# A two-block transformer layer in fp32: branch gates moved into the stick attention, gather, merge and trunk in one phase, heads turned ahead of the scores

## The chip, the cores and the metric

The kernel runs on one core of one Trainium2 chip. TensorE (PE) multiplies matrices into PSUM; VectorE (DVE), ScalarE (ACT) and GpSimd (POOL) do the elementwise work, GpSimd on SBUF alone; SyncE's queue (SPq) issues all DMAs. The metric is the time of one execution in microseconds.

## The reference, cut to what matters

`x` has 1024 tokens of 1024 features. Only the end of the first block and the attention of the second are touched.

```python
# first block, after o_a (gated delta rule, 4 heads of 128) and o_b (stick-breaking attention, 8 heads of 64)
o_a = _rms(o_a, dn_out_gain).reshape(b, s, 512) * jax.nn.silu(z_a)
y_a = jnp.einsum('bsc,cd->bsd', o_a, w_up_a)
o_b = o_b * jax.nn.silu(z_b)
y_b = jnp.einsum('bsc,cd->bsd', o_b, w_up_b)
gates = jax.nn.sigmoid(proj[..., B_Z1:G1] + b_gate)
merged = gates[..., :1024] * y_a + gates[..., 1024:] * y_b
x = x + jnp.einsum('bsd,de->bse', merged, w_out)
# second block: z = rms_norm(x, g) @ w_in, then 8 heads of softmax attention over latents (MLA)
# and 4 heads of differential attention (two softmaxes a head, the second taken off with a weight)
```

Products keep fp32 precision by splitting both factors into a high part of a shorter format and the rest: each product is three matmuls, hi x hi, hi x lo and lo x hi. ScalarE writes `hi` (a copy into the shorter format), VectorE writes `lo` (a subtraction).

## The kernel before, in words

The program is a row of phases. A phase owns its SBUF, PSUM and semaphores; at its end all engines meet at a barrier, and only then does the next one issue its first DMA. Inside a phase, `run_stages` takes stages (classes with one generator for each engine) and a plan, a list of stage numbers: each engine runs through the same plan and takes one step of the stage named. Each engine executes its own stream in order; stages are tied by semaphores alone. A wait at the head of an engine's stream holds all that comes after it in that stream.

**The stick phase** (682 to 1049 us of the profile). `StickAttention` has 64 units, 8 token tiles j of 8 heads h; a unit's keys grow from 128 (tile 0) to 1024 (tile 7). For unit i: TensorE's `score` (L579 to L581), ScalarE's two sigmoids (L504, L507), VectorE's scan (L553) and product (L528), TensorE's transposes `flip` two steps later (L590), ScalarE's copy into `weight_t` (L517), TensorE's `apply` (L603). `give` copies the tile's outputs out of PSUM (L535), which are stored to `o_b`. Between the units, by `even_plan`, `GateProjection` computes the merge gates (L717 to L719, 16 weight tiles of 4 steps of 12 matmuls of 512 columns) and stores `gates`. It has one raw weight buffer; a tile's split (L678, L697) stands three steps ahead of its use.

**The gather phase** (1050 to 1117). Two rounds of four token tiles. Each loads `o_a`, `o_b`, `z_a`, `z_b`, normalises and gates them (L1484 to L1525: square, sum, square root, reciprocal, four products, SiLU), transposes them on TensorE (L1539), and splits them into `branches` (L1492, L1530).

**The merge phase** (1117 to 1221). `project_merge` goes over 4 chunks of 256 output features with both up projections, `features_products` (L186): 384 matmuls of 512 columns, two in a row with the same weights. Gates are multiplied in over all 1024 tokens (L1604), added (L1606), split (L1585, L1611) into `merged`.

**The trunk phase** (1221 to 1530). `WeightRing` streams weights through two raw and two split slots (L2466, L2474, L2479); `OutProject` (through `token_products`, L2521 to L2523) multiplies `merged` with `w_out`, token tile by token tile; `InProject` and the latents follow.

**The attend phase** (1531 to 1914). `attention_plan` interleaves two units of `MlaAttention` with one of `DiffAttention`. Both share two PSUM slots `t` for transposes and two slots `z` for scores. In a step TensorE does `score`, then `turn` (the next tile's queries or keys transposed into a `t` slot, L2020 and L375), `flip` (transposes of the softmax of two units ago, L2040 and L2322; a unit of more than 512 keys takes both `t` slots), and `apply`. Of a turned slot ScalarE writes the high part (L1880, L385) and, in `DiffAttention`, VectorE the rest (`keep_lo`, L398 and L401), which frees it. VectorE's `top` (L1963, L2241) takes the maximum and frees `z`.

Of the kernel before, what the change touches and what calls it, by code (L numbers as in the profile page):

```python
# [16 lines left out]
P = 128  # L17
# [42 lines left out]
def slot_loop(eng, n, step, straight=False):  # L60

    rounds = (n - 1) // 2
    if rounds >= 2 and not straight:
        with eng.Fori(0, rounds) as t:
            for s in range(2):
                step(t, s, True)
    else:
        for t in range(rounds):  # L70
            for s in range(2):
                step(t, s, True)
    for c in range(2 * rounds, n):
        step(c // 2, c % 2, c + 1 < n)


# [3 lines left out]


class WeightStore:

    def __init__(self, nc, stack, name, size):
        sb = lambda n, w, dtype: stack.enter_context(nc.sbuf_tensor(f"{name}_{n}", [P, w], dtype))
        self.raw = sb("w_raw", size, F32)
        self.hi = [sb(f"w_hi{s}", size, F32R) for s in range(2)]
        self.lo = [sb(f"w_lo{s}", size, F32R) for s in range(2)]  # L90

    def views(self, kt, width, pieces):
        view = lambda t: t[:, 0:kt * width].rearrange("p (k n) -> p k n", n=width)
        raw, kp = view(self.raw), kt // pieces
        return [raw[:, h * kp:(h + 1) * kp] for h in range(pieces)], [view(t) for t in self.hi], [view(t) for t in self.lo]


class Weights:

    def __init__(self, ph, kt, width, source, pieces=2, store=None, ready=False, following=None, goes_on=None):
        self.nc, self.width, self.pieces, self.source = ph.nc, width, pieces, source
        self.kp = kt // pieces
        if store:
            self.raw, self.hi, self.lo = store.views(kt, width, pieces)
        else:
            self.raw = [ph.sb(f"w_raw{h}", [P, self.kp, width])[:] for h in range(pieces)]  # L110
            self.hi = [ph.sb(f"w_hi{s}", [P, kt, width], F32R)[:] for s in range(2)]
            self.lo = [ph.sb(f"w_lo{s}", [P, kt, width], F32R)[:] for s in range(2)]

        self.goes_on = goes_on
        if goes_on:
            self.loaded, self.hi_done, self.lo_done, self.used, self.before = (
                goes_on.loaded, goes_on.hi_done, goes_on.lo_done, goes_on.used, goes_on.before)
        else:
            self.loaded = ph.sem2("w_loaded", pieces)
            self.hi_done = ph.sem2("w_hi_done", pieces)  # L120
            self.lo_done = ph.sem2("w_lo_done", pieces)
            self.used = ph.sem2("w_used")
            self.before = 1 if ready else 0
        self.next = None
        if following:
            kt, width, first = following
            self.next = Weights(ph, kt, width, lambda c, h: first(0, h), pieces, store, goes_on=self)

    def load(self, sp, t, s, width=None):
        w = width or self.width  # L130
        for h in range(self.pieces):
            if not isinstance(t, int) or 2 * t + s > self.before:

                for other in (range(self.pieces) if self.goes_on else (h,)):
                    sp.wait_ge(self.lo_done[other], 2 * t + s - self.before)
            source = self.source(2 * t + s, h) if w == self.width else self.source(2 * t + s, h, w)
            sp.dma_start(self.raw[h][:, :, 0:w], source).then_inc(self.loaded[h], 16)

    def split_hi(self, act, t, s, width=None):
        w = width or self.width  # L140
        act.wait_ge(self.used[s], t)
        for h in range(self.pieces):
            act.wait_ge(self.loaded[h], 16 * (2 * t + s + 1 - self.before))
            k = slice(h * self.kp, (h + 1) * self.kp)
            self.nc.scalar.activation(self.hi[s][:, k, 0:w], self.raw[h][:, :, 0:w],
                                      ACT.Copy).then_inc(self.hi_done[h], 1)

    def split_lo(self, dve, t, s, width=None):
        w = width or self.width
        for h in range(self.pieces):  # L150
            dve.wait_ge(self.hi_done[h], 2 * t + s + 1 - self.before)
            k = slice(h * self.kp, (h + 1) * self.kp)
            self.nc.vector.tensor_tensor(self.lo[s][:, k, 0:w], self.raw[h][:, :, 0:w],
                                         self.hi[s][:, k, 0:w].bitcast(F32),
                                         ALU.subtract).then_inc(self.lo_done[h], 1)

    def begin(self, do, eng, width=None):

        if not self.before:
            do(eng, 0, 0, width)  # L160

    def stream(self, more):

        return self if more else self.next

    def wait_split(self, pe, t, s):
        if isinstance(t, int) and 2 * t + s < self.before:
            return
        for h in range(self.pieces):
            pe.wait_ge(self.lo_done[h], 2 * t + s + 1 - self.before)  # L170

def next_item(t, s):

    return (t, 1) if s == 0 else (t + 1, 0)

def features_products(nc, out, hi, lo, w_hi, w_lo, kt, ch):  # L180

    for k in range(kt):
        for weight, part, first in ((w_hi, hi, True), (w_hi, lo, False), (w_lo, hi, False)):
            for half in range(2):
                cols = slice(half * HALF, (half + 1) * HALF)
                last = nc.tensor.matmul(out[:, cols], weight[:, k, ch], part[:, k, cols],  # L186
                                        start=(k == 0 and first), stop=(k == kt - 1 and weight is w_lo))
    return last
# [221 lines left out]
class StickAttention:  # L410
# [4 lines left out]
    def __init__(self, ph, nc, src, v, q_gain, k_gain, out, c):  # L415
        self.nc, self.v, self.out, self.c = nc, v, out, c
# [39 lines left out]
    def sync(self, sp):  # L456
# [8 lines left out]
        for i in range(self.steps()):  # L465
            if self.next_tile(i, 0) is not None:
                self.prep.load(sp, self.next_tile(i, 0))
            if i >= len(self.units):
                yield
                continue  # L470
            j, h = self.units[i]
            if h == 5 and j:
                store(j - 1)
            yield
# [46 lines left out]
    def vector(self, dve):  # L521
# [101 lines left out]
class GateProjection:  # L623
# [21 lines left out]
    def sync(self, sp):  # L645
        def load(i):
            if i:
                sp.wait_ge(self.lo_done, i)
# [25 lines left out]
    def split_hi(self, act, i):  # L674
        act.wait_ge(self.loaded, 16 * (i + 1))
        if i >= 2:
            act.wait_ge(self.summed, 2 * (i - 1))
# [3722 lines left out]
```

## Time and profile before

| | us |
|---|---|
| median of 3 runs (lowest, highest) | 2894.46 (2893.68, 2897.53) |
| the profiled execution, its own time | 2896.21 |
| its span, first to last instruction | 2894.5 |
| busy in the span: PE, DVE, ACT, POOL | 2618.9, 1267.4, 947.8, 278.1 |
| mean granted TensorE clock | 0.955 of full |

All times of the profile are counted from the start of its span. A row of the timeline is: start, duration, engine, line, operation, out<-in, shape, count, and in brackets the idle time of the engine before it and what ended it. Durations of matmuls overlap (a 512-column matmul lasts 0.39 us and the next one starts 0.23 us after it), so the pace is read from the starts. A row of busy time by stretch is: start and end, length, then busy us and instructions of TensorE, of its weight loads, of VectorE, ScalarE and GpSimd, the granted TensorE clock, the share of the DMA engines, GB/s. A row of a group is: line, engine, operation, out<-in, shape, count | busy us, mean ns | idle us before it and what ended it. A row of waits is: who waited for whom, us in total, times, longest.

### The profile page before, as it was taken

To read this page: it belongs to the slowest core of one execution; us is meant where nothing else is said; L and a number is where in the kernel's file an instruction comes from. 1 tells how busy PE (TensorE), PEld (TensorE's weight loads), DVE (VectorE), ACT (ScalarE), POOL (GpSimd) and SP (SyncE) were. 2 spreads that over 40 slices of the span, in tenths; PEclk is the share of its full clock that TensorE was granted. 3 is DMA by queue.
4 is the path that set the end of the run, shared out by engine and by line. 5 is a ranking of instruction groups with operands and counts; after the bars stand their busy time and mean duration, and the time that the engine had idled before them with its cause. 6 is when DMAs were issued, how large, how long until landed. Compare 5 with 4: busy or idle time off the path is not lost. (4 is left out here: it accounts for less than half of the span.)

```text
span 2894.5 us, 36626 instructions
## 1 busy us (share of the span) xinstructions
PE 2618.9 (90%) x14702; PEld 2245.7 (78%) x14702; DVE 1267.4 (44%) x1770; ACT 947.8 (33%) x1539; POOL 278.1 (10%) x393
## 2 busy tenths in 40 slices
PE   8969999995999955799994888979999999999999
PEld 6859999995888844688893676768788888888877
DVE  5523444432566544434124866645323323333443
ACT  4223222211456532123112766633211111122331
POOL 1002222210001000001002312111000000000000
PEclk9989999997999987999995998989999999999999
DMA  4231212102322124343235111034321221255532
GB/s 139 81 99 57 77 50 61 56 27 83 92 67 64 47 77 142 119 151 118 82 110 173 43 37 49 17 134 142 84 74 66 76 77 51 84 202 180 184 104 84
DMA packets 220256, 264.71 MB, mean 91 GB/s; under 512 B 54677, under 2 KB 153621, under 8 KB 220089
## 3 DMA queue, kind: packets, MB, share of 16 engines
q1 hardware_dynamic: 220088, 262.38, 28.4%
q8 instruction: 117, 1.92, 0.3%
q14 instruction: 51, 0.41, 0.0%
HBM read 185.11 MB, written 77.22 MB: 91 GB/s over the span
## 5 line engine op out<-in xcount | busy, mean ns | idle before, releaser
L3590 PE MATMUL ffn_up_acc<-mixed_hi,ffn_ring_hi 128*128 128x512 f32 x704 | 274.3, 390 | 2.5 <-DVE mixed_lo L2742 2.5
L3590 PE MATMUL ffn_up_acc<-mixed_hi,ffn_ring_lo 128*128 128x512 f32 x704 | 273.9, 389 | 0.0
L3590 PE MATMUL ffn_up_acc<-mixed_lo,ffn_ring_hi 128*128 128x512 f32 x704 | 273.9, 389 | 0.0
L1419 PE MATMUL delta_acc<-delta_w_hi,xn_hi 128*128 128x256 f32 x640 | 191.5, 299 | 2.9 <-DVE delta_w_lo L1373 2.9
L1421 PE MATMUL delta_acc<-delta_w_hi,xn_lo 128*128 128x256 f32 x640 | 181.1, 283 | 0.0
L1420 PE MATMUL delta_acc<-delta_w_lo,xn_hi 128*128 128x256 f32 x640 | 180.9, 283 | 0.0
L2521 PE MATMUL trunk_acc<-trunk_ring_hi,merged_hi 128*128 128x512 f32 (+1 forms) x384 | 149.7, 390 | 16.1 <-DVE trunk_ring_lo L2479 16.1
L3590 PEld LDWEIGHTS ffn_up_acc<-mixed_hi,ffn_ring_hi 128*128 128x128 f32 x704 | 132.1, 188 | 30.1 <-issue 2.9
L3590 PEld LDWEIGHTS ffn_up_acc<-mixed_hi,ffn_ring_lo 128*128 128x128 f32 x704 | 132.1, 188 | 27.6
L3590 PEld LDWEIGHTS ffn_up_acc<-mixed_lo,ffn_ring_hi 128*128 128x128 f32 x704 | 132.1, 188 | 27.2
L2522 PE MATMUL trunk_acc<-trunk_ring_lo,merged_hi 128*128 128x512 f32 (+1 forms) x384 | 147.8, 385 | 0.0
L2523 PE MATMUL trunk_acc<-trunk_ring_hi,merged_lo 128*128 128x512 f32 (+1 forms) x384 | 147.6, 384 | 0.0
L3849 DVE TENSOR_TENSOR ffn_feed_lo<-ffn_feed_raw,ffn_feed_hi 128x1536 fp32r<-128x1536 f32 x44 | 77.4, 1759 | 147.1 <-ACT ffn_feed_hi L3841 147.1
L3560 DVE TENSOR_SCALAR ffn_conv<-ffn_padded,ffn_taps 128x1024 f32<-128x1024 f32 x22 | 16.6, 753 | 274.8 <-ACT ffn_padded L3541 274.8
L1419 PEld LDWEIGHTS delta_acc<-delta_w_hi,xn_hi 128*128 128x128 f32 x640 | 122.0, 191 | 8.9 <-issue 5.5
L1420 PEld LDWEIGHTS delta_acc<-delta_w_lo,xn_hi 128*128 128x128 f32 x640 | 122.1, 191 | 0.0
L1421 PEld LDWEIGHTS delta_acc<-delta_w_hi,xn_lo 128*128 128x128 f32 x640 | 121.8, 190 | 0.0
L3541 ACT ACTIVATE ffn_padded<-ffn_up_acc 128x1024 f32<-128x1024 f32 x22 | 22.6, 1028 | 301.4 <-PE ffn_up_acc L3590 301.4
L553 DVE TENSOR_TENSOR_SCAN stick_keep<-stick_keep,stick_zero 128x127 f32<-128x127 f32 (+7 forms) x64 | 86.7, 1354 | 78.3 <-ACT stick_keep L504 77.7
L3841 ACT ACTIVATE ffn_feed_hi<-ffn_feed_raw 128x1536 fp32r<-128x1536 f32 x44 | 65.4, 1487 | 159.5 <-PE ffn_up_acc L3917 159.5
L717 PE MATMUL stick_g_acc<-xn_hi,stick_g_hi 128*128 128x512 f32 x256 | 107.3, 419 | 6.0 <-DVE stick_g_lo L697 5.6
L3917 PE MATMUL ffn_up_acc<-ffn_feed_hi 128*128 128x512 f32 x352 | 108.8, 391 | 0.0
(431 smaller groups left out, 6236.2 us busy)
## 6 DMA issues: line engine op xcount, KB each, us to landing
ffn_feed_raw<-in_w_down SPq DMA_DIRECT2D x44, 512.0 KB, 4.1
ffn_ring_raw<-in_w_gate SPq DMA_DIRECT2D x11, 1024.0 KB, 5.4
ffn_ring_raw<-in_w_up SPq DMA_DIRECT2D x11, 1024.0 KB, 5.8
scratch_act_t<-ffn_silu SPq DMA_DIRECT2D x22, 512.0 KB, 2.6
ffn_feed_raw<-scratch_act_t SPq DMA_DIRECT2D x44, 256.0 KB, 3.0
delta_w_raw<-in_w_in SPq DMA_DIRECT2D x20, 512.0 KB, 4.0
scratch_projected<-delta_out SPq DMA_DIRECT2D x80, 128.0 KB, 1.7
stick_g_raw<-in_w_in SPq DMA_DIRECT2D x16, 512.0 KB, 4.5
```

Source lines behind the costliest of these rows:

```text
L553: nc.vector.tensor_tensor_scan(back, back, self.zero[:].to_broadcast([P, n - 1]), 1.0, ALU.mult, ALU.add).then_inc(self.scanned, 1)
L717: nc.tensor.matmul(self.acc[:], w_hi, self.hi[:, k, cols], start=(k == 0), stop=False, skip_group_check=True)
L1419: nc.tensor.matmul(acc, self.hi[:, k, tok], w_hi, start=(k == 0), stop=False, skip_group_check=True)
L1420: nc.tensor.matmul(acc, self.hi[:, k, tok], w_lo, start=False, stop=False, skip_group_check=True)
L1421: last = nc.tensor.matmul(acc, self.lo[:, k, tok], w_hi, start=False, stop=(k == self.kt - 1), skip_group_check=True)
L2521: nc.tensor.matmul(out, hi[:, k, tok], w_hi, start=(k == 0), stop=False)
L2522: nc.tensor.matmul(out, hi[:, k, tok], w_lo, start=False, stop=False)
L2523: last = nc.tensor.matmul(out, lo[:, k, tok], w_hi, start=False, stop=(k == kt - 1))
L3590: last = nc.tensor.matmul(self.acc[s][:, br, cols], weight[:, k, ch], part[:, k, cols], start=(k == 0 and first), stop=(k == 7 and weight ...
L3841: self.nc.scalar.activation(self.hi[s][:], self.raw[s][:], ACT.Copy).then_inc(self.hi_done[s], 1)
L3849: self.nc.vector.tensor_tensor(self.lo[s][:], self.raw[s][:], self.hi[s][:].bitcast(F32), ALU.subtract).then_inc(self.lo_done[s], 1)
L3917: last = nc.tensor.matmul(t.pairs[j][:, half, :], part, weight[:, HALF + half * HALF:HALF + (half + 1) * HALF], start=begins, stop=ends, s ...
```

## The change

Three edits.

1. **Gates inside the stick phase.** `BranchGates`, a third stage, runs 8 steps for each token tile beside the stick's 8 units. It normalises and gates `o_a` mostly on GpSimd, and leaves `silu(z_b)` in the stick's output tile, with which `give` multiplies the output. Both halves go to one tensor `gated`. SiLU becomes a sigmoid and a product. `even_plan` puts its step behind each stick step. The stick's store moves from unit 5 to unit 4. `GateProjection` gets two raw buffers that lie on its `lo` buffers; its loads wait for the tile before to be summed, and the split stands two steps ahead of its use.
2. **One trunk phase.** `BranchGather` (load `gated`, transpose, split), `MergeWeights` (the up weights, through the ring's buffers) and `Merge` (16 units: half of the tokens by 128 features, both branches) replace the two phases, ahead of the trunk's stages. Behind merge units 12 and 13 (of 0 to 15) stand the ring's first two splits. `TokenHalves` lets later tensors take the place of dead halves; `turn` has two slots instead of one.
3. **Turn first.** In both attentions, TensorE's `turn`, ScalarE's `keep` and (`DiffAttention`) VectorE's `keep_lo` move to the front of the step.

```diff
@@ StickAttention.vector, give
-            if j:
-                dve.wait_ge(self.stored, 16 * j)
-            nc.vector.tensor_copy(self.o_sb[:], self.o[:]).then_inc(self.o_out, 1)
+            dve.wait_ge(self.gates.silu_b, j + 1)
+            nc.vector.tensor_tensor(self.o_sb[:], self.o_sb[:], self.o[:], ALU.mult).then_inc(self.o_out, 1)
@@ GateProjection.sync
         def load(i):
-            if i:
-                sp.wait_ge(self.lo_done, i)
+            if i >= 2:
+                sp.wait_ge(self.summed, 2 * (i - 1))
@@ BranchGates (new): scalar, vector, gpsimd; s is the step in the tile
+                if s == 0:
+                    act.wait_ge(self.o_in, 16 * (j + 1))
+                    if j:
+                        act.wait_ge(self.silu_b, j)
+                    nc.scalar.activation(self.sig[:], self.per_head(), ACT.Square).then_inc(self.squared, 1)
+                if s == 2:
+                    act.wait_ge(self.z_a_in, 16 * (j + 1))
+                    act.wait_ge(self.summed, j + 1)
+                    nc.scalar.activation(self.sig[:], self.z[:], ACT.Sigmoid).then_inc(self.sig_a, 1)
+                if s == 5:
+                    act.wait_ge(self.z_b_in, 16 * (j + 1))
+                    nc.scalar.activation(self.sig[:], self.z[:], ACT.Sigmoid).then_inc(self.sig_b, 1)
...
+                if s == 1:
+                    self.nc.vector.tensor_reduce(self.total[:], ...).then_inc(self.summed, 1)
...
+                if s == 1:   # GpSimd: mean and power -0.5 of 128x4, then two products of 128x512
+                if s == 3:   # two products of 128x512
+                if s == 6:   # one product of 128x512, z * sig into the stick's o_sb
@@ even_plan
-        plan.append(0)
+        plan += [0, 2]
@@ Merge.tensor (new), a unit (half, j)
+            for branch in range(2):
+                key = ("merge", u, branch)
+                self.acc.wait_free(pe, key)
+                for k in range(4):
+                    nc.tensor.matmul(out, w_hi[:, k, ch], hi, start=(k == 0), stop=False)
+                    nc.tensor.matmul(out, w_hi[:, k, ch], lo, start=False, stop=False)
+                    last = nc.tensor.matmul(out, w_lo[:, k, ch], hi, start=False, stop=(k == 3))
+                self.acc.fill(last, key)
@@ merge_plan (new), ahead of trunk_plan
+    plan = [gather, gather, weights, gather, weights, gather]
+    for u in range(16):
+        plan += [weights, weights] * (u in (0, 2, 4))
+        plan += [weights] * (u == 8)
+        plan += [gather] * (4 <= u < 8)
+        plan += [merge]
+        plan += [ring] * (u in (12, 13))
+    return plan + [merge]
@@ MlaAttention.tensor, DiffAttention.tensor
-            if i < self.nu:
-                score(i)
             for s in range(2):
                 ...
                     turn(...)
+            if i < self.nu:
+                score(i)
```

`BranchGather.sync` issues tile 0, tile 1, the first weights, tile 2, the second weights; tile 3 waits until tile 0 is transposed (three buffers). `Merge.vector` does two products of 128x512 with the sums, an addition and, one unit later, the subtraction.

## Rows read from the trace of the kernel before

**Rows 1.** The page's section on DMA issues: KB each, us to landing.

```profile
ffn_feed_raw<-in_w_down SPq DMA_DIRECT2D x44, 512.0 KB, 4.1
```

**Rows 2.** Busy time by stretch; clock in parts of full speed.

```profile
711.00:1046.00 335.00, 328.88 (x1986) 285.82 (x1986) 192.73 (x191) 173.91 (x303) 20.47 (x12) 0.99 0.22 63
1046.00:1231.00 185.00, 100.30 (x450) 83.94 (x449) 84.99 (x97) 50.12 (x57) 0.10 (x1) 0.79 0.36 128
1231.00:1527.00 296.00, 294.41 (x1383) 251.87 (x1384) 88.02 (x108) 66.17 (x125) 16.75 (x49) 0.99 0.35 119
1574.00:1912.00 338.00, 292.98 (x1912) 242.68 (x1912) 222.34 (x604) 215.87 (x501) 77.17 (x116) 0.95 0.13 36
```

**Rows 3.** TensorE in order of time, 1045 to 1239 us.

```profile
1045.65 0.39 PE L719 MATMUL stick_g_acc<-xn_hi,stick_g_lo 128*128 128x512 f32 x1
...
1125.49 1.19 PE L186 MATMUL merge_acc<-branches_hi,merge_w_hi 128*128 128x512 f32 x2 [11.12 <-DVE merge_w_lo L153]
...
1214.18 0.61 PE L186 MATMUL merge_acc<-branches_hi,merge_w_lo 128*128 128x512 f32 x2
1230.94 0.80 PE L2521 MATMUL trunk_acc<-trunk_ring_hi,merged_hi 128*128 128x512 f32 x1 [16.15 <-DVE trunk_ring_lo L2479]
...
1235.91 0.40 PE L2521 MATMUL trunk_acc<-trunk_ring_hi,merged_hi 128*128 128x512 f32 x1
...
1238.67 0.39 PE L2521 MATMUL trunk_acc<-trunk_ring_hi,merged_hi 128*128 128x512 f32 x1
```

**Rows 4.** SyncE's queue and ScalarE in order of time, behind the stick attention.

```profile
1050.43 0.33 SPq L1470 DMA_DIRECT2D gather_gain<-in_dn_out_gain  x1
...
1059.28 0.63 ACT L1484 ACTIVATE gather_square<-gather_o 128x512 f32<-128x512 f32 x1 [2.06 <-DMA gather_z<-scratch_projected]
```

**Rows 5.** Groups by line and shape, 1046 to 1231 us.

```profile
L1530 DVE TENSOR_TENSOR branches_lo<-gather_t,branches_hi 128x1024 f32 x8 | 9.4, 1219 | 3.9 <-ACT branches_hi L1492 3.9
...
L1492 ACT ACTIVATE branches_hi<-gather_t 128x1024 f32 x8 | 7.9, 1023 | 11.3 <-PE gather_t L1539 11.3
...
L1501 DVE TENSOR_REDUCE gather_stat<-gather_square 128x4 f32<-128x512 f32 x8 | 5.5, 686 | 32.6 <-ACT gather_square L1484 32.6
...
L2474 ACT ACTIVATE trunk_ring_hi<-trunk_ring_raw 128x2048 fp32r<-128x2048 f32 x2 | 3.8, 1909 | 8.0 <-DMA trunk_ring_raw<-in_w_out 8.0
...
L2479 DVE TENSOR_TENSOR trunk_ring_lo<-trunk_ring_raw,trunk_ring_hi 128x2048 fp32r<-128x2048 f32 x1 | 2.3, 2292 | 7.9 <-ACT trunk_ring_hi L2474 7.9
```

**Rows 6.** The stick attention in order of time: TensorE, SyncE's queue, ScalarE.

```profile
694.24 1.97 PE L375 MATMUL stick_t<-ident,stick_prep_xn 128*128 128x128 f32 x8 [15.82 <-DVE stick_prep_xn L365]
...
708.38 0.42 SPq L649 DMA_DIRECT2D stick_g_raw<-in_w_in  x1
...
713.87 1.06 ACT L678 ACTIVATE stick_g_hi<-stick_g_raw 128x1024 fp32r<-128x1024 f32 x1 [1.81 <-DMA stick_g_raw<-in_w_in]
```

**Rows 7.** Single lines, shortest, median, longest ns: VectorE beside GpSimd.

```profile
L1140 DVE TENSOR_TENSOR delta_upper<-delta_mt,delta_mask x8: 681/1090/1091, 233.3 to 598.3; 128x512 f32<-128x512 f32 x8
...
L1142 DVE TENSOR_TENSOR delta_upper<-ident,delta_upper x8: 693/1664/1670, 234.0 to 599.4; 128x512 f32<-128x512 f32 x8
...
L1161 POOL TENSOR_TENSOR delta_bt<-delta_mt,delta_mask x40: 1260/1286/1744, 225.8 to 621.6; 128x512 f32<-128x512 f32 x40
```

**Rows 8.** GpSimd's groups by shape: a power of 128x4.

```profile
L3393 POOL TENSOR_TENSOR ffn_mixed_inverse<-ffn_mixed_mean,ffn_mixed_half 128x4 f32<-128x4 f32 x8 | 8.1, 1011 | 0.7
```

**Rows 9.** What TensorE waited for, 1574 to 1912 us.

```profile
PE attend_mla_acc L2053 <- DVE attend_mla_o L1975: 10.7, 7, 2.1
...
PE attend_t L2322 <- DVE attend_diff_prep_k L401: 9.4, 6, 2.1
PE attend_t L2322 <- DVE attend_diff_prep_q_lo L398: 8.4, 6, 1.8
```

**Rows 10.** TensorE in the attention, waits in a long and a short tile.

```profile
1713.04 0.55 PE L2322 MATMUL attend_t<-ident,attend_diff_probs 128*128 128x128 f32 x3 [1.51 <-DVE attend_diff_prep_q_lo L398]
...
1598.45 0.88 PE L2030 MATMUL attend_z<-attend_mla_k_t,attend_mla_q_t 96*128 96x384 f32 x2 [1.07 <-DVE attend_diff_neg_top L2241]
```

More of the change, by code:

```diff
@@ L98 @@
[L98 to L170, printed above, removed]
@@ L174, in next_item @@
[L174 to L188, printed above, removed]
@@ L660, in sync @@
         for i, half, part in self.walk():
-            if half == 1 and part == 0 and i + 2 < self.tiles:
-                load(i + 2)
+            if half == 0 and part == 1 and 2 <= i + 1 < self.tiles:
+                load(i + 1)
             if part == 0 and 2 * i + half >= 1:
@@ L683, in scalar @@
         for i, half, part in self.walk():
-            if half == 0 and part == 1 and i + 1 < self.tiles:
+            if half == 1 and part == 0 and i + 1 < self.tiles:
                 self.split_hi(act, i + 1)
@@ L702, in vector @@
         for i, half, part in self.walk():
-            if half == 0 and part == 1 and i + 1 < self.tiles:
+            if half == 1 and part == 0 and i + 1 < self.tiles:
                 self.split_lo(dve, i + 1)
@@ L1633, with merge_plan @@
+def merge_plan():
+    gather, weights, merge, ring = range(8, 11), None, None, 0
+    gather, weights, merge = 8, 9, 10
+    plan = [gather, gather, weights, gather, weights, gather]
[6 more added lines that the diff above has]
+    return plan + [merge]
 MLA_H, NOPE, ROPE, MLA_V, Q_RANK, KV_RANK = 8, 64, 32, 64, 256, 128
@@ L1903, in scalar @@
         for i in range(self.steps()):
+            for s in range(2):
+                if self.following(i, 3 * s, 1) is not None:
+                    keep(self.following(i, 3 * s, 1), s)
             if self.following(i, 1) is not None:
@@ L2218, in scalar @@
         for i in range(self.steps()):
+            for s in range(2):
+                if self.following(i, s, 1) is not None:
+                    keep_hi(self.following(i, s, 1), s)
             if self.following(i, 0) is not None:
@@ L2222, in scalar @@
                 weigh(i - 1)
-            for s in range(2):
-                if self.following(i, s, 1) is not None:
-                    keep_hi(self.following(i, s, 1), s)
             if 0 <= i - 2 < self.nu:
@@ L2284, in vector @@
                 give(self.units[u][0])
+            for s in range(2):
+                if self.following(i, s, 1) is not None:
+                    self.prep.keep_lo(dve, self.following(i, s, 1), s)
             if i < self.nu:
@@ L2288, in vector @@
                 invert(i - 1)
-            for s in range(2):
-                if self.following(i, s, 1) is not None:
-                    self.prep.keep_lo(dve, self.following(i, s, 1), s)
             if self.following(i, 0) is not None:
@@ L2760, with __init__ @@
     N = 4
-    def __init__(self, ph, nc, acc):
-        self.nc, self.acc, self.tiles, self.number = nc, acc, [ph.sb(f"out{b}", [P, HALF]) for b in range(self.N)], {}
+    def __init__(self, ph, nc, acc, place):
+        self.nc, self.acc, self.tiles, self.number = nc, acc, [place.sb(f"out{b}", [P, HALF]) for b in range(self.N)], {}
         self.stored = ph.sem2("stored", self.N)
```

580 lines of the change are left out of this document (327 added, 253 removed).

## The prediction

> **What bounds the kernel now.** I read the page first: a span of 2894.5 us, and TensorE busy in 90% of it. An average over stages does not say what one stage is worth, so the next view is busy time by stretch [rows 2]. In the stick attention (711 to 1046) TensorE is busy 328.9 of 335 us, in the trunk (1231 to 1527) 294.4 of 296: both are TensorE's, and work of other engines there costs only if it stops TensorE. Between them, 1046 to 1231, TensorE is busy 100.3 of 185 us. In the attention (1574 to 1912) it is 293.0 of 338. These two stretches are where the change can win. The third view is TensorE's order of time [rows 3]: the stick's last matmul ends at 1046.0, the merge's first starts at 1125.49, its last two at 1214.18, the trunk's first at 1230.94. So the stretch is a gap of 79.4 us (64 transposes lie in it), 89.3 us of matmuls, and a gap that the bracket puts at 16.15 us and ends with the ring's `lo`. The fourth view is what TensorE waited for in the attention [rows 9].
>
> **Term 1, the gap behind the stick attention.** What stays is the barrier: the last matmul ended at 1046.0, and the first DMA of the next phase went out at 1050.43 [rows 3, 4]; after the change this DMA is tile 0 of `gated`. What goes: squares, sums, roots, products and SiLU of both rounds, the second round's loads, and the merge phase's own start. What comes is a chain of four tiles and two weight pieces of 512 KB each. A load of 512 KB lands in 4.1 us [rows 1]. When loads are queued, the next square of the gather came after 2.06 us of idle time and the 0.63 of the one before, for 1 MB of its tiles [rows 4]: 1.35 us for each further 512 KB. Eight transposes at the low clock took 1.97 us [rows 6]; a `hi` of 128x1024 takes 1.02 and a `lo` 1.22 [rows 5]; I add 0.1 for each hand-over.
> Tile 0 lands at 1054.5, is transposed at 1056.5, has its `hi` at 1057.7 and its `lo` at 1059.0. Tile 1 is transposed at 1058.5, its `lo` ends at 1061.0. The first weights follow (`lo` at 1062.2), then tile 2, which needs tile 0's slot (transposed at 1061.1, `lo` at 1063.6), then the second weights (1064.8). Tile 3's load is issued at 1056.5 behind three others and lands at about 1061.3; transposed at 1063.5, `hi` at 1064.7, `lo` at 1066.0. The first merge matmul starts at 1066.2. Bounds: VectorE's six `lo` in a row from 1057.8 end at 1065 even if no load holds, and if tile 3's load takes double the time it is 1071.
>
> **Term 2, the merge.** The same 384 matmuls of 512 columns. They came every 0.23 us, two with the same weights; now each has its own, as in the trunk, where twelve took 2.76 us, 0.230 each [rows 3]. I take 0.232: 89.1 us. The transposes of tiles 4 to 7 stand between units, 32 at half of the low clock's price [rows 6]: 3.9 us. The start at the low clock: the trunk's first twelve took 4.97 us instead of 2.76 [rows 3], 2.2 us too much (the granted clock of the whole stretch is 0.79 [rows 2], so parts of it ran at the lower level, 1.2 GHz). Sum 95.2 us, end at 1161.4. What could hold it: a unit is 24 matmuls, 5.6 us. VectorE's unit is four passes of 128x512 of 0.69 (the length of L1501 [rows 5]): 2.8 us. In units 4 to 7 a `lo` of 1.22 comes on top and in unit 4 two more, 6.5 us at most against 6.5 with the transposes, and four accumulators lie between. ScalarE has half of that. If VectorE did hold units 4 to 7 by 1 us each, it is 4 us.
>
> **Term 3, the gap ahead of the trunk.** It goes: the ring's first splits (`hi` 1.91, `lo` 2.29 [rows 5]) are ordered behind merge units 12 and 13. Counted from the end of unit 12: VectorE's products and sum 2.2, `hi` to 4.8, `lo` to 7.2; the next pair to 15.0. The trunk's first product can start at 16.8 and needs the second piece 2.8 later. Behind this `lo` on SyncE's queue stands the load of the last unit's gates: issued at 15.1, landed by 19, used at 19. The trunk's first four token tiles, 22 us, need the first half of the tokens only, so the last unit's `hi` and `lo` have cover; without it they would cost 5 us. The trunk's own start at the low clock, 2.2 us, goes too.
> So the trunk's matmuls are ahead by 1230.94 + 2.2 - 1161.4 = 71.7 us. From there the trunk is TensorE's, and does the same.
>
> **Term 4, what the stick attention pays.** Its start: three more DMAs (0.42 us each on the queue) are issued ahead of the first gate weights, and these hold ScalarE and TensorE: issued at 708.38, split at 713.87 [rows 6]. So 1.3 us, with the bytes 1.6. Then, for each tile: ScalarE three passes of 128x512 (0.63 each [rows 4]), VectorE one reduction of 0.69 [rows 5] (the product in `give` takes the copy's place), GpSimd a mean, a power (1.0 [rows 8]) and five products. ScalarE is busy 173.9 and VectorE 192.7 of 335 us [rows 2], 2.7 and 3.0 in a mean unit of 5.2, and `flip` comes two steps after its score, so these are covered; if the cover were gone they would cost 15 and 5.5 us. GpSimd's products read SBUF beside VectorE. What this does was measured in the delta phase [rows 7]: one VectorE product of two SBUF tensors took 681 ns at the shortest and 1090 in the middle, the one behind it 693 and 1664; both stand where L1161 runs on GpSimd. The two together lose 1.38 us, about one GpSimd product (1.29). Forty such products could take 40 x 1.29 = 52 us from VectorE; it would then be busy 250 of 335. A burst of two (2.6) is a little more than the 2.2 us that VectorE has free in a mean unit. I take 1 us for the phase beyond the start: 2.6 in all; bounds 1.3 and 20.
> The Trainium skill (GPSIMD Engine Reference, Key points) says that GpSimd shares its SBUF interfaces with VectorE and contends with VectorE instructions that have two SBUF inputs. By that rule each product and subtraction of two SBUF tensors in the stick's VectorE stream may be stretched; the trace agrees for the pair of lines in [rows 7]. The third rival below takes this to its end.
>
> **Term 5, the attention.** TensorE waited at `flip` for slots that turned heads still held: 9.4 and 8.4 us, twelve waits at L2322 [rows 9]. One of them: the second half of a flip waits 1.51 us for `keep_lo` [rows 10]. With the turn ahead of the scores (eight matmuls of 512 columns at this length, 1.9 us) the slot is free in time. Against it: VectorE now does `keep_lo` (0.7) before `top`, so `z` is freed later, and ScalarE's exponentials wait for the turn. In short tiles TensorE already waits for `z`, 1.07 us at 1598.45 [rows 10]. Bounds: all of the 17.8 us, or a loss of 0.7 in each of 32 units less what the slots give back, about -8. I take 70% of the waits, 12.5 us, as ScalarE (216 of 338) and VectorE (222 [rows 2]) have room, above all in the long tiles, where the waits are.
>
> **Sum.** 71.7 - 2.6 + 12.5 = 81.6. The profiled execution took 2896.2 us, 1.7 over the median of the runs. 2896.2 - 81.6 = 2814.6; against the median, 2813.
>
> **Rivals.**
> *The attention gives nothing.* The slot wait becomes one for `z` or for the exponentials. For it: VectorE's order is strict, and TensorE's longest wait there (10.7, for `give` [rows 9]) stays. Against it: the room above. 2825; at the bound of -8, 2833.
> *All of it comes.* Attention 17.8, stick 1.3: 2806.
> *GpSimd takes the stick's slack.* Half of the 52 us reaches TensorE: 2838; all of it, 2863. Against it: TensorE idles only 6 of 335 us now, and VectorE has 142 us free there.
> *Slower than before.* ScalarE's sigmoid of `z_b` at step 5 waits for a load that waits for GpSimd's gated tile: square 0.6, sum 0.7, mean and power 1.2, four products of 1.3, a load of 3 to 4: together 12 us from step 0. All the sigmoids of the scores stand behind it. Five mean units are 26 us. It decides only from there on; to eat 82 us it must take 10 us in each of 8 tiles, a chain of 36 us. Nothing in the rows is so long.
>
> **Chances.** The forecast 0.55, with its own range 2809 to 2820; the attention gives nothing 0.24; all of it comes 0.06; the stick pays more 0.11; slower 0.03; no change 0.01. A run of this kernel can tell 0.2%, 6 us, from no change. Faster 0.96, same 0.01, slower 0.03. The range takes the attention's two bounds and 5 to 8 us for the first and fourth term: 2798 to 2838.
>
> **What would show it.** The first merge matmul 20 us after the stick's last (term 1); 16 units of 5.6 us with no wait (term 2); no idle time between merge and trunk (term 3); the stick's stretch within 3 us of before, and no ScalarE wait for the sigmoid's load (term 4); the slot waits of L2322 gone, and no larger wait for `z` (term 5). The prediction is wrong above all if ScalarE or SyncE's queue stands still in the stick attention for GpSimd.

## The result and the profile after

The changed kernel takes 2808.97 us (median of 4 runs, 2806.64 to 2815.80), the kernel before on the same chip 2894.07 (4 runs): a ratio of 0.9709, 95% interval 0.9689 to 0.9729. Forecast were 2813 and faster, a gain of 81.6 us; by these medians it is 85.1. The execution that was profiled is the longest of the four: its own time is 2815.8, its span 2814.1.

The spans differ by 80.4 us. By stretch, each measured between the same two instructions in both traces:

| stretch | before | after | gain | forecast |
|---|---|---|---|---|
| start to the stick's first scan | 711.0 | 712.4 | -1.4 | 0 |
| first scan to the stick's last matmul | 335.0 | 342.2 | -7.2 | -2.6 |
| to the trunk's first matmul (`w_out`) | 184.9 | 113.8 | 71.1 | 69.5 |
| trunk, first to last matmul | 296.2 | 291.5 | 4.8 | 2.2 |
| to the attention's first `top` | 46.4 | 45.5 | 0.9 | 0 |
| first to last `top` | 322.9 | 306.3 | 16.6 | 12.5 |
| to the ffn's first turn | 21.8 | 21.8 | 0.0 | 0 |
| the rest | 976.2 | 980.6 | -4.4 | 0 |

Busy time by stretch, of the changed kernel, answering to [rows 2]:

```profile
712.40:1054.70 342.30, 330.30 (x1986) 286.31 (x1986) 213.27 (x199) 186.49 (x328) 97.86 (x68) 0.98 0.29 86
1054.70:1168.40 113.70, 100.04 (x448) 83.13 (x449) 62.41 (x77) 28.59 (x34) 0.10 (x1) 0.91 0.52 178
1168.40:1464.40 296.00, 291.86 (x1385) 250.35 (x1383) 89.67 (x113) 67.60 (x126) 16.68 (x49) 1.00 0.35 119
1506.00:1827.20 321.20, 291.31 (x1908) 244.82 (x1907) 220.15 (x604) 215.36 (x501) 76.87 (x116) 0.93 0.13 37
```

In the stick attention VectorE is busy 213.3 us, 20.5 more than before, and has only 5.4 us more to do (eight sums): 15.1 us are the same instructions taking longer. Between stick and trunk TensorE's 100 us of work now fill 113.7.

TensorE in order of time, of the changed kernel, answering to [rows 3]:

```profile
1062.57 3.68 PE L1474 MATMUL trunk_turn<-ident,trunk_gated 128*128 128x128 f32 x16 [7.93 <-DMA trunk_gated<-scratch_gated]
1067.88 1.07 PE L1474 MATMUL trunk_turn<-ident,trunk_gated 128*128 128x128 f32 x8 [1.63 <-DMA trunk_gated<-scratch_gated]
1070.53 1.94 PE L1474 MATMUL trunk_turn<-ident,trunk_gated 128*128 128x128 f32 x8 [1.59 <-DMA trunk_gated<-scratch_gated]
1075.05 0.77 PE L1635 MATMUL trunk_acc<-trunk_branches_hi,trunk_ring_hi 128*128 128x512 f32 x1 [2.57 <-DVE trunk_branches_lo L1461]
...
1168.19 0.39 PE L1637 MATMUL trunk_acc<-trunk_branches_hi,trunk_ring_lo 128*128 128x512 f32 x1
1168.41 0.39 PE L2545 MATMUL trunk_acc<-trunk_ring_hi,trunk_merged_hi 128*128 128x512 f32 x1
```

The stick's last matmul ends at 1054.64. The first merge matmul comes 20.4 us later, and the first of the trunk 0.22 us behind the last of the merge, at full pace.

The start of the stick attention, of the changed kernel, SyncE's queue, ScalarE, VectorE and TensorE, answering to [rows 6]:

```profile
709.78 0.43 SPq L627 DMA_DIRECT2D stick_a_o<-scratch_o_a  x1
710.25 0.43 SPq L630 DMA_DIRECT2D stick_a_z<-scratch_projected  x1
710.74 0.42 SPq L633 DMA_DIRECT2D stick_a_gain<-in_dn_out_gain  x1
711.20 0.43 SPq L526 DMA_DIRECT2D stick_g_raw<-in_w_in  x1
...
717.85 1.06 ACT L554 ACTIVATE stick_g_hi<-stick_g_raw 128x1024 fp32r<-128x1024 f32 x1 [2.17 <-DMA stick_g_raw<-in_w_in]
...
718.94 1.98 DVE L573 TENSOR_TENSOR stick_g_lo<-stick_g_raw,stick_g_hi 128x1024 fp32r<-128x1024 f32 x1 [1.70 <-ACT stick_g_hi L554]
...
720.97 0.79 PE L593 MATMUL stick_g_acc<-xn_hi,stick_g_hi 128*128 128x512 f32 x1 [8.95 <-DVE stick_g_lo L573]
```

Tile 3's first units, of the changed kernel, in order of time, VectorE, then GpSimd, then TensorE:

```profile
824.27 2.31 DVE L426 TENSOR_TENSOR_SCAN stick_keep<-stick_keep,stick_zero 128x511 f32<-128x511 f32 x1
826.50 1.70 DVE L402 TENSOR_TENSOR stick_chance<-stick_chance,stick_keep 128x511 f32<-128x511 f32 x1
828.23 0.69 DVE L408 TENSOR_TENSOR stick_o<-stick_o,stick_o_acc 128x512 f32<-128x512 f32 x1
...
824.20 1.30 POOL L691 TENSOR_TENSOR stick_a_o<-stick_a_o,stick_a_gain 128x512 f32<-128x512 f32 x1
825.64 2.01 POOL L696 TENSOR_TENSOR stick_a_o<-stick_a_o,stick_a_z 128x512 f32<-128x512 f32 x1
827.73 1.60 POOL L699 TENSOR_TENSOR stick_a_o<-stick_a_o,stick_a_sig 128x512 f32<-128x512 f32 x1
...
829.07 1.08 PE L476 MATMUL stick_o_acc<-stick_v,stick_weight_t 128*128 128x64 f32 x8 [1.10 <-DVE stick_o L408]
```

A scan of 511 elements beside no GpSimd product takes 1.22 us, the product behind it 0.67; here they take 2.31 and 1.70. The product in `give` (L408) stands behind them in VectorE's stream, and TensorE's `apply` (L476) waits for it.

What TensorE waited for in the attention, of the changed kernel, from first to last `top`, answering to [rows 9] (who waited for whom, us, times, longest):

```profile
PE attend_mla_acc L2077 <- DVE attend_mla_o L1999: 11.6, 9, 2.1
PE attend_z L2336 <- DVE attend_mla_neg_top L1987: 7.7, 1, 7.7
PE attend_z L2054 <- DVE attend_diff_neg_top L2265: 5.6, 6, 1.9
PE attend_t L2346 <- DVE attend_diff_prep_k L275: 3.4, 2, 2.2
PE attend_t L2346 <- DVE attend_diff_prep_q_lo L272: 0.8, 1, 0.8
```

The 17.8 us of waits for turned heads at the Diff flip (now L2346) are 4.2.

What TensorE waited for behind the attention, of the changed kernel; the row has no counterpart in the profile of before:

```profile
PE ffn_up_acc L3943 <- DVE ffn_emb L3729: 4.0, 1, 4.0
```

This is code that the change doesn't touch: VectorE's copy waits there for a store to land. The wait comes back in later profiles (3.5 us in scores_first, 2.6 in after_again, 1.1 in by_tile). In the twelve later profiles, all with the same ffn, the stretch takes 972.6 to 979.2 us, 975.9 in the mean, around the 976.2 of before. So the 4.4 us of the table's last row belong to this execution, and so do the 1.4 of its first row: in all thirteen profiles with changed code the first scan lies at 709.2 to 713.3, around the 711.0 of before.

### The profile page after: what moved, and what is told of

The parts are those of the page before. It is cut to its first block and busy times, and to the rows that moved or that the text cites. A ratio compares the mean times of both kernels' runs of the same rounds, so it can differ in the third digit from the quotient of the medians.

```text
span 2814.1 us, 36540 instructions
## 1 busy us (share of the span) xinstructions
PE 2620.0 (93%) x14702; PEld 2249.0 (80%) x14702; DVE 1263.9 (45%) x1762; ACT 939.3 (33%) x1541; POOL 352.9 (13%) x450
## 5 line engine op out<-in xcount | busy, mean ns | idle before, releaser
L3586 DVE TENSOR_SCALAR ffn_conv<-ffn_padded,ffn_taps 128x1024 f32<-128x1024 f32 x22 | 16.6, 753 | 276.4 <-ACT ffn_padded L3567 276.4
L3943 PE MATMUL ffn_up_acc<-ffn_feed_lo,ffn_feed_hi 128*128 128x512 f32 x352 | 109.3, 392 | 0.0
L3943 PE MATMUL ffn_up_acc<-ffn_feed_hi,ffn_feed_lo 128*128 128x512 f32 x352 | 109.3, 392 | 0.0
L594 PE MATMUL stick_g_acc<-xn_lo,stick_g_hi 128*128 128x512 f32 x256 | 101.8, 398 | 0.0
```

The source lines that it names most:

```text
L594: nc.tensor.matmul(self.acc[:], w_hi, self.lo[:, k, cols], start=False, stop=False, skip_group_check=True)
L3943: last = nc.tensor.matmul(t.pairs[j][:, half, :], part, weight[:, HALF + half * HALF:HALF + (half + 1) * HALF], start=begins, stop=ends, s ...
```

## The experiments

Every change below is made to the changed kernel. Four stretches are read, each between fixed instructions: the stick from first to last scan (315.3 us before, 322.4 after), the start from the first scan to the first gate matmul (5.2, 8.5), the merge from its first matmul to the trunk's first (93.4 after), the attention from first to last `top` (322.9, 306.3).

**scores_first.** Edit 3 undone.

```diff
@@ tensor, both attentions (keep and keep_lo likewise)
+            if i < self.nu:
+                score(i)
             for s in range(2):
                 ... turn(...)
-            if i < self.nu:
-                score(i)
```

> The changed kernel with edit 3 undone: in both attentions the scores come before the turn again, ScalarE's keep behind the exponentials, VectorE's keep_lo behind top and invert. Measured from the first to the last top of the attention, the kernel before takes 323.0 us and the changed one 306.4. Theory: all of these 16.6 us are the order, so this kernel takes 323.0 +- 0.5 and about 16.6 us more in all (2825), and TensorE's waits for slots at flip return to about 18 us. Rival: part of the gain comes from where the phase starts or from its transfers; then the stretch stays under 320.

Attention 322.0 us; 2823.45 in all (4 runs, 2823.39 to 2823.77). TensorE's waits, in scores_first:

```profile
PE attend_t L2346 <- DVE attend_diff_prep_k L275: 9.4, 6, 2.1
PE attend_t L2346 <- DVE attend_diff_prep_q_lo L272: 8.4, 6, 1.8
PE attend_t L2064 <- DVE attend_diff_prep_q_lo L272: 2.9, 3, 1.3
...
PE attend_t L2064 <- ACT attend_mla_k_t L1904: 2.4, 7, 0.3
...
PE attend_t L2064 <- ACT attend_mla_q_t L1904: 2.0, 6, 0.3
```

The order is the whole gain of the attention. 17.8 us of waits are back at the Diff flip, and 7.3 at the Mla flip (L2064), which the prediction had not counted.

**diff_only.** Turn first in `DiffAttention`, `MlaAttention` as in scores_first.

> Turn first in DiffAttention alone, MlaAttention has its order of before. The slot waits named in the kernel before are those of the Diff flips for the Diff heads' keep_lo. Theory: they are the whole gain, so the stretch from first to last top takes 306 to 309 us. Rival: MlaAttention's turn, which no row of before names as a releaser, has its share; then it takes 310 to 316.

Attention 314.0 us (2811.89 in all, one run): half of the way. The theory of the slot waits of L2322 alone falls, its rival holds. The share is an estimate from one profile: its granted clock was 0.77 in the first 60 us, like the changed kernel's 0.76 and below the 0.83 of before. So the 7.7 us to the changed kernel compare like with like, and the 8.9 to the kernel before are likely some 3 too few (long_only, below, shows such a loss of 3 us). The Mla flip still waits for its own turned heads (4.9 us at L2064, 0.4 in the changed kernel), and the Mla score for a `z` that a Diff score holds (12.0 us at L2054, 5.6 in the changed kernel).

**keep_lo_last.** Only VectorE's part of edit 3 undone.

```diff
@@ DiffAttention.vector
-            (keep_lo of the next tile)
             if i < self.nu:
                 top(i)
             if 0 <= i - 1 < self.nu:
                 invert(i - 1)
+            (keep_lo of the next tile)
```

> Only VectorE's keep_lo of DiffAttention goes back behind top and invert; TensorE's turn and ScalarE's keep stay in front. In the changed kernel VectorE idles 2.24 us ahead of a keep_lo of a short tile and top stands behind it. Theory that the late z costs the short tiles: the stretch gets shorter than 306.4, to about 303. Rival: the slot is freed only by keep_lo, so the slot waits at flip return; then it takes 312 or more.

Attention 346.4 us, 40 more than the changed kernel and 23 more than before (2846.78 in all). TensorE's waits, in keep_lo_last:

```profile
PE attend_t L2346 <- DVE attend_diff_prep_q_lo L272: 13.3, 6, 3.6
PE attend_t L2346 <- DVE attend_diff_prep_k L275: 13.1, 6, 3.6
...
PE attend_t L2044 <- DVE attend_diff_prep_k L275: 8.5, 8, 2.0
```

These 40 us are far outside the 8 us by which this stretch differs between executions (long_only, below). The slot is taken earlier and freed no earlier. The rival of the expectation holds, and more strongly than written: turn first without `keep_lo` first is worse than neither.

**long_only.** Both orders: turn first where a unit has more than 512 keys, scores first in the short ones.

> Turn first only in units of more than 512 keys, the order of before in the short ones, in both attentions. Against the kernel before, the changed one loses 3.3 and 3.0 us in the two series of short tiles and gains 11 and 8 us in the two series of long ones. Theory that these are separate: 306.4 - 6.3 = 300 us from first to last top, and 6 us less in all. Rival: the loss of the short tiles comes from the switch between orders or from what a tile hands on to the next; then 304 to 308.

Attention 303.9 us; 2805.08 in all (4 runs, 2802.68 to 2807.61). Taken alone this is 2.4 us better than the changed kernel. It is not shown: eight profiles with exactly the changed kernel's attention (those of the other experiments that leave it alone, too) take 300.3 to 308.2 us, so it lies among them. Busy time in the first 60 us of the attention, in the changed kernel:

```profile
1505.34:1565.34 60.00, 47.33 (x240) 38.60 (x241) 42.97 (x152) 38.53 (x107) 19.68 (x31) 0.76 0.17 47
```

The same stretch in a second profile of the same kernel (after_again, below):

```profile
1502.01:1562.01 60.00, 46.23 (x261) 36.92 (x262) 45.66 (x157) 40.41 (x112) 20.03 (x31) 0.85 0.18 50
```

The same code gets a mean clock of 0.76 of full in one execution and 0.85 in the other, and does 240 and 261 matmuls. Behind a wait of 2.1 us that both have (for `give`), the first stood at 0.50, 1.2 GHz, from 1530 to 1538, and the second was back at 0.98 in the 4 us that answer to it. There the first falls 3.1 us behind and stays so. The 3.3 us that the short tiles seemed to lose against the kernel before are the clock's. A second such place lies 169 us behind the first `top`: in the 20 us from there after_again has a clock of 0.91 and does 102 matmuls, no_products has 0.76, does 93 and falls 3 us behind. Why the clock differs there is open.

**no_products.** GpSimd's four products of 128x512 in a tile are cut to 128x4, so the normalisation and the gate of `o_a` are left out. One of the four:

```diff
-                    nc.gpsimd.tensor_tensor(self.o[:], self.o[:], self.inverse[:].unsqueeze(2).to_broadcast(shape), ALU.mult
+                    nc.gpsimd.tensor_tensor(self.mean[:], self.total[:], self.half[:], ALU.mult
...
```

> The changed kernel, with the four GpSimd products of 128x512 per tile in BranchGates cut to products of 128x4 (normalisation and gate of o_a are left out; the product into the stick's output tile, all loads, all waits, ScalarE's and VectorE's passes stay). From the first to the last scan the kernel before takes 315.3 us, the changed one 321.6 to 322.4 in five profiles. Theory: GpSimd's products stretch VectorE's scan and product in units 2 to 4 of a tile, give is late, and TensorE's next apply waits: the 3.4 us behind the start go, about 318.3 to 319, and no wait for stick_o is left; the start stays. Rival: the waits come from ScalarE's passes and the longer queues; then 321.5 and the waits for stick_o stay.

Stick 318.5 us, start 7.8. TensorE's waits from the first scan on, in no_products:

```profile
PE stick_g_acc L593 <- DVE stick_g_lo L573: 8.2, 1, 8.2
PE stick_g_acc L593 <- ACT stick_gate L567: 0.4, 2, 0.3
PE stick_o_acc L476 <- ACT stick_weight_t L391: 0.2, 1, 0.2
```

The waits for `stick_o` (2.4 us in the changed kernel) are gone, and from unit 3 on every scan keeps its distance to the kernel before within 0.3 us. Behind unit 3 the changed kernel falls back by another 3.5 us, this one by none: that is what GpSimd's products cost, and the start is the rest.

**chain_later and chain_behind.** The chain of each tile two steps later. chain_behind was to issue the first loads behind the gate weights', in step 1; but the gate projection's first step stands behind that one in the plan, so its queue is that of chain_later, and it counts as a second profile of it.

```diff
@@ BranchGates, steps of the tile
-    square 0, sum and two products 1, sigmoid z_a 2, two products 3, z_b 4, sigmoid z_b 5, last product 6, next loads 7
+    square 2, sum and two products 3, sigmoid z_a 4, two products 5, z_b 6, sigmoid z_b 7, last product 7, next loads 8
```

> Nothing is left out; BranchGates' chain is two steps later in each tile (square at 2, sum at 3, mean, power and two products at 3, sigmoid of z_a at 4, two products at 5, z_b at 6, last product at 7), so that GpSimd's products run while units 4 to 7 are scanned and not ahead of give at step 2. Theory: as many VectorE instructions are stretched, but nobody waits behind them: 318.3 to 319.2 from first to last scan, the start as in the changed kernel. Rival: VectorE's slack is used up wherever the products are; then it stays at 321 or more.

> As chain_later, and BranchGates' first three loads are issued behind the first loads of the gate weights. From the first scan to the first matmul of the gate projection the kernel before takes 5.2 us, the changed one 7.7 to 8.5. Theory: three issues of 0.42 ahead on the queue, the bytes of two more loads and a subtraction that runs beside GpSimd (1.98 us, 1.22 before) make this; here it is 5.2 to 5.6, and first to last scan 315.3 to 316.2. In all 6 us less than the changed kernel, about 2803. Rival: only the queue's 1.3 us come back; then 317.

Stick 323.5 and 323.3 us: no better. From tile 3 on the theory holds, no scan falls further behind by more than 0.1 us. VectorE is stretched no less: its 64 scans and 64 products take 151.6 us in chain_later, 147.3 in the changed kernel and 134.4 in no_products. Yet no wait for `stick_o` is left, so it is the place of the stretch that costs TensorE time, and not its amount. But at the first scans of tiles 1 and 2 the kernel loses 2.0 and 2.1 us, and 0.7 at tile 2's end. SyncE's queue in tile 0, in chain_later:

```profile
737.45 0.34 SPq L531 DMA_DIRECT2D scratch_gates<-stick_gate  x1
743.66 0.32 SPq L641 DMA_DIRECT2D stick_a_z<-scratch_projected  x1
744.03 0.43 SPq L642 DMA_DIRECT2D scratch_gated<-stick_a_o  x1
744.50 0.43 SPq L526 DMA_DIRECT2D stick_g_raw<-in_w_in  x1
```

TensorE, in chain_later:

```profile
753.69 0.66 PE L249 MATMUL stick_t<-ident,stick_prep_xn 128*128 128x128 f32 x4 [1.64 <-DVE stick_prep_q_lo L272]
```

The load of `z_b` waits 6 us for GpSimd; behind it stands the load of the gate weights, 6.3 us later than in the changed kernel (738.18). ScalarE's split waits for it (3.24 us at 750.54), behind the split stands the head's high part, and TensorE waits. This is the head-of-line chain of the prediction's slower rival, at 2 us a tile where tiles are short. In all chain_later took 2803.70 (one run), chain_behind 2806.67 (4 runs, 2803.99 to 2811.74). The profiled executions, 2803.70 and 2811.74, differ by 8.0 us, of which the attention, 301.1 and 308.2, makes 7.1.

**ring_last.** The ring's first two splits behind the last merge unit.

```diff
         plan += [merge]
-        plan += [ring] * (u in (12, 13))
-    return plan + [merge]
+    return plan + [merge] + [ring] * 2
```

> The trunk ring's first two splits stand behind the last merge unit and not behind units 12 and 13. From the first merge matmul to the first of the trunk the changed kernel takes 92.1 to 93.4 us with no idle time ahead of the trunk. Theory: the place of the splits, not the missing barrier alone, is worth time: the last unit's products (2.8), its hi and lo (1.3) and the ring's hi and lo (1.9 and 2.3) come in a row, a gap of about 8 us, and the trunk's first 12 matmuls are at the lower clock again (2.2): 100 to 104 us. Rival: VectorE and ScalarE are ahead, so the gap is under 3 us.

Merge 100.1 us, and the trunk 2.4 longer (293.9) with its first matmuls at 1.2 GHz again. TensorE, in ring_last:

```profile
1174.33 0.77 PE L2544 MATMUL trunk_acc<-trunk_ring_hi,trunk_merged_hi 128*128 128x512 f32 x1 [6.38 <-DVE trunk_ring_lo L2502]
```

So of the 76 us gained to the trunk's end, 9 hang on where two splits stand, with no barrier between merge and trunk (2820.47 in all, one run).

**on_vector.** The four products on VectorE, two behind `give`'s place in step 2, two in step 3.

> The changed kernel with BranchGates' four products of 128x512 a tile on VectorE (behind give in step 2, and in step 3) instead of GpSimd; nothing is left out. VectorE gets 32 x 0.69 = 22 us more of its own and loses about 15 us of stretch. Theory: four unstretched products behind give cost TensorE nothing, so first to last scan takes 318 to 319 us, as with the products left out (318.5), and no wait for stick_o is left. Rival: 2.8 us in a row hold the scan of the next unit longer than GpSimd's stretch did; then 322 or more, with waits for chance or prep.

Stick 318.4 us, start 7.6, no wait for `stick_o` (2800.19 in all, one run). No scan behind unit 3 stays further behind than that one. So 22 us of VectorE's own, unstretched, cost TensorE nothing, and about 15 us of stretch in the wrong place cost 3.5.

**by_tile, by_tile_long, after_again.** by_tile puts together what held: the late chain in tiles 3 to 7, the early one in tiles 1 and 2, and in tile 0 the loads at step 2, behind the gate weights', with the late chain and its second pair of products at step 4. `FIRST`, `SHORT` and `LONG` hold the steps. by_tile_long adds long_only. after_again is the changed kernel.

```diff
@@ BranchGates
+    def at(self, j):
+        return self.FIRST if j == 0 else self.SHORT if j < 3 else self.LONG
...
@@ sync, tile 0
+                if j == 0 and s == 2:
+                    load_o(0)
+                    load_z(0)
```

> Nothing is left out. BranchGates' chain stands two steps later in tiles 3 to 7, as in the changed kernel in tiles 1 and 2, and in tile 0 its loads are issued behind the first loads of the gate weights, its square two steps later and its gate products a step ahead of the stick's own GpSimd step. In the changed kernel the scans fall behind those of before by 3.65 us in units 0 to 2, 0.44 and 0.23 in tiles 1 and 2, 2.8 from tile 3 on; with the whole chain later they fall 2.0 and 2.1 behind at the start of tiles 1 and 2 and next to nothing from tile 3 on. Theory: these are three separate causes (start: queue and bytes; short tiles: a load queued behind a chain; long tiles: GpSimd beside VectorE ahead of give), so first to last scan takes 315.3 + 0.1 + 0.4 + 0.2 = 316 us, first matmul of the gate projection 5.2 to 5.6 after the first scan. Rival: the start's delay is bytes only and comes back with the loads behind, in unit 3 or 4; then 318 or more.

> by_tile's stick attention and long_only's attention order. In five profiles of kernels with the changed kernel's attention the stretch from first to last top takes 301.1 to 308.2 us, in long_only 303.9. Theory that the order of the short tiles is worth 2 to 3 us: about 302 us here and 2 us less in all than by_tile. Rival: it is worth nothing; then the stretch lies anywhere from 301 to 308 and the totals are within 2 us.

> The changed kernel unchanged, beside by_tile and by_tile_long on the same chip: 2807 to 2811. By the theory by_tile is 6 us below it, by the rival 3. Its profile says which of the stretches (attention 301 to 308 us, the emb stores in the ffn, 4 us in one profile) differ from one execution to the next.

Stick 316.4 us, start 5.3 in by_tile: the theory's 316, and with the loads behind the gate weights' the start is back at that of the kernel before (5.2). TensorE's waits from the first scan on, in by_tile:

```profile
PE stick_g_acc L593 <- DVE stick_g_lo L573: 5.7, 1, 5.7
PE stick_g_acc L593 <- ACT stick_gate L567: 0.4, 2, 0.3
PE stick_o_acc L476 <- DVE stick_o L408: 0.2, 1, 0.2
```

by_tile 2799.01 us (5 runs, 2795.18 to 2803.64), ratio to the kernel before 0.9668 (0.9647 to 0.9688); after_again 2807.39 (2801.18 to 2808.87), 0.970 (0.9682 to 0.9718); by_tile_long 2803.56 (2794.22 to 2804.97), 0.9677 (0.9655 to 0.9699). The medians put by_tile 8 us below the changed kernel; the stick stretch of the profiles gives 5.1 to 6.1 of them. The two profiled executions themselves, 2800.68 and 2801.18, are only 0.5 apart, as after_again's attention was the shortest of all. The two intervals overlap, so that by_tile beats the changed kernel is shown in the stretch, and likely in the whole. long_only's order adds nothing that can be seen: the attention took 302.5 beside 304.4 and 300.3, and by_tile_long's median is 4.6 above by_tile's, where the theory wanted 2 below.

## Why the prediction was right, and where its terms were off

The forecast of 2813 lies 4 us above the measured median. The mechanisms and the largest term were right; that the total is so near is in part luck, as the misses of the others nearly cancel: the stick paid 4.6 us more than forecast, and 4.2 more were gained to the trunk's end, 4.1 more in the attention, 0.9 at its opening, against 4.4 and 1.4 lost in untouched code of the profiled execution. 81.6 - 4.6 + 4.2 + 4.1 + 0.9 - 4.4 - 1.4 = 80.4.

**Term 1** stands. Forecast were 20.2 us from the stick's last matmul to the merge's first, measured 20.4, and 18.6 to 21.6 in the later profiles. The first tile's transposes began 7.9 us behind the stick's end (forecast 8.5), the later ones were held by transfers, as the rows above show: two more waits for `gated`, 1.63 and 1.59 us. The `lo` of tile 3 was the last to end.

**Term 2** was 1.9 us too high: 93.4 us instead of 95.2. A unit of 24 matmuls took 5.44 us where no transposes stand, 0.227 a matmul, not 0.232; units 3 to 6, each with eight transposes, 6.24 to 6.36; the first 2.7 more at the low clock. VectorE never held it.

**Term 3** stands. No idle time ahead of the trunk, and ring_last shows that it is the order that removes it. What the term left out lies in the trunk: besides 2.2 us of low clock, the trunk gained 0.5, 0.8 and 0.8 us at three places where transposes had waited for the subtraction that frees the single `turn` slot (0.36, 0.59 and 0.65 us in the profile of before) and now wait no more. The change's list has the second slot; the prediction said that the trunk does the same. No run tests the slot by itself.

**Term 4** was mis-sized: 7.2 us instead of 2.6. The start took 3.65: 1.4 on the queue as forecast, 1.2 for a landing in 6.65 us instead of 5.49, 0.75 because `g_lo` ran beside GpSimd (1.98 instead of 1.23), and 0.3 at the low clock, at which the first twelve gate matmuls took 4.99 us instead of 4.66. Of the last three only the bytes had been given a share, of 0.3. In six other profiles with the same stick phase the start took 2.65 to 2.99 and the whole term 6.2 to 6.6: the landing was 6.34 to 6.58 us, and `g_lo` ran beside GpSimd in one of them only. So up to 1 us of the 7.2 is this execution's. Beyond the start 3.5 us instead of 1, in units 3 and 4 of the tiles. The bound for VectorE was right in kind (15.1 us of at most 52); the step that failed is "a little more than the 2.2 us that VectorE has free in a mean unit". A mean unit doesn't decide; the unit ahead of `give` does, since TensorE waits for that one within the step: waits for `stick_o` alone are 2.4 us, in four tiles. by_tile moves the products off it in tiles 3 to 7 and gets 2.9 us back; no_products takes them away and gets 3.5.

The prediction weighed the rule of the Trainium skill on shared interfaces. The Trainium skill's page SBUF — State Buffer (SBUF: two separate sides) says more: the shared pair is an exclusive lock, and whichever starts first, a GpSimd instruction that reads SBUF or a VectorE instruction with two SBUF inputs, holds it for the whole instruction while the other one blocks. The rows of tile 3 agree. The scan begins at 824.27, the GpSimd product L691 holds on until 825.50, and from there 1.22 us make 826.7, near the scan's end of 826.58; the next GpSimd product in its turn lasts 2.01 instead of 1.28. And L408, with one input in PSUM, takes 0.69 beside L699, as it does in tile 7, where no GpSimd product runs beside it.

**Term 5** was too low: 16.6 us in the profiled execution, and 18.8 in the mean of eight profiles (304.1), above the bound of 17.8. That bound took the waits at one line, L2322, as all there was. scores_first shows 7.3 us more at the Mla flip, and diff_only that the order of `MlaAttention`, to which the prediction's sum gave no share, is worth about 8 us of it. The loss that the prediction set against it (`z` freed later) didn't come (its bound of -8 can't be redone: 0.7 in 32 units is 22.4, and what the slots give back is given by no row): 13.9 us of waits for `z` before (10.6 and 3.3), 13.3 after. VectorE does stand at `keep_lo` (31 us for `q_hi`, 5 before), and had the room.

**The rivals.** That the attention gives nothing is refuted. That GpSimd takes the stick's slack is right in mechanism and a seventh of its size. The slower one's chain exists, as chain_later shows in the short tiles, at 2 us where it needed 10. That no ScalarE wait for the sigmoid's load would appear was right for the changed kernel; it waits once, 1.6 us, for the load of the first square.

What stays open: why the granted clock of the attention differs between executions, why the transfers of the merge's opening differ by 3 us between profiles, and how much of by_tile's 8 us beyond its 5 to 6 in the stick is chance.

## What to carry to other kernels

Bound the price of GpSimd's work beside VectorE's not by the mean slack of a stage but at the one instruction that another engine waits for within the step, and place the disturbing work behind it. When a slot passes through three engines, move the steps of all three together: here, taking it earlier without freeing it earlier cost 23 us against the kernel before. Count every line that waits for a shared slot, not the one with the largest wait. And where a stage leaves TensorE short idle times, profile the unchanged kernel twice before a difference of 3 us is given a cause.

## What the runs showed of the hardware that was not expected

TensorE's granted clock in the first 60 us of the attention was 0.74 to 0.85 in mean in eight profiles of the same code, and the stretch from first to last `top` took 308.2 us in the one with 0.74 and 300.3 to 304.4 in the four with 0.85. VectorE's scan, whose second operand is one broadcast column, is stretched beside GpSimd's products like an instruction with two full SBUF inputs: 2.31 us instead of 1.22. The product with one input in PSUM (L408) stood beside a GpSimd product in seven of its eight executions and took 0.686 to 0.690 us in all of them.
